# Modulation weights laid out so that each partition's share of a quarter is one contiguous row

## The reference, cut to what matters

```
def ada_params(cond_act, w, b):
    mod = cond_act @ w + b
    return jnp.split(mod, 3, axis=-1)

act_lat = jax.nn.silu(c)          # [1, 1024]
act_ctx = jax.nn.silu(c_ctx)      # [1024]
for i in range(DEPTH):            # 2 layers; w_ada[i] is [1024, 3072]
    sh_l, sc_l, gt_l = ada_params(act_lat, w_ada[i], b_ada[i])
    u_lat = rms_norm(h_lat, norm_g[i]) * (1.0 + sc_l[:, None, :]) + sh_l[:, None, :]
    sh_c, sc_c, gt_c = ada_params(act_ctx, w_ada[i], b_ada[i])
    ...
```

## Time and profile before

| | |
|---|---|
| median of 3 runs | 1286.72 us (1286.43 to 1286.76) |
| profiled execution, its own time | 1288.5 us |
| its span | 1286.7 us, 17486 instructions |
| PE busy | 1272.4 us (99%) |
| DVE / ACT / POOL busy | 64% / 51% / 35% |
| DMA | 135.44 MB in 181402 packets, mean 105 GB/s |
| in the first 40 us | 13.45 MB in 7944 packets, mean 336 GB/s |
| granted TensorE clock | 1.00 in every stretch of 40 us and of 2 us looked at |

### The profile page before, as it was taken

How to read it: one execution, slowest core, us unless ns; L and a number is a source line. 1 busy time by engine, 2 the same in 40 slices (tenths; PEclk the granted TensorE clock), 3 DMA queues, 4 the chain that set the end, 5 groups by cost and what they waited for, 6 DMA issues and landing times.

```text
span 1286.7 us, 17486 instructions
## 1 busy us (share of the span) xinstructions
PE 1272.4 (99%) x6553; PEld 1065.8 (83%) x6553; DVE 822.9 (64%) x1216; ACT 655.6 (51%) x1074; POOL 447.7 (35%) x212
## 2 busy tenths in 40 slices
PE   8999999999999999999999999999999999999998
PEld 4688888889988888888789889888888888888886
DVE  1796788764945447789658436406448668667686
ACT  4543777844523354766655534633355534545341
POOL 0234011137432394522244233344563322333310
PEclk9999999999999999999999999999999999999999
DMA  9972001066332153321223333233354243332301
GB/s 347 306 256 74 11 23 33 18 235 196 98 99 65 34 164 99 98 54 62 65 73 93 82 82 83 67 97 98 98 158 154 85 128 99 105 109 82 115 1 66
DMA packets 181402, 135.44 MB, mean 105 GB/s; under 512 B 10155, under 2 KB 154652, under 8 KB 181325
## 3 DMA queue, kind: packets, MB, share of 16 engines
q1 hardware_dynamic: 181122, 134.34, 34.5%
q10 hardware_dynamic: 202, 0.06, 0.0%
HBM read 129.66 MB, written 4.72 MB: 104 GB/s over the span
## 4 chain that ended last, share of the span: by engine, by line
PE 84%; DVE 6%; ACT 4%; DMA 3%; issue 2%; POOL 1%; SPq 0%; DVEq 0%; ACTq 0%; POOLq 0%
PE psum L2373 26%; PE psum L2375 25%; PE psum L2374 25%; PE psum L2587 2%; DMA ada_w<-in_w_ada 1%; DMA w_raw<-in_fno_w_in 1%; PE psum L2431 1%; PE psum L2575 1%; PE psum L2576 1%; DVE out_rows L2306 1%; POOL w_lo L784 1%; ACT w_hi L903 1%; DVE m_probs L2029 0%; DVE m_turned_lo L2034 0%; PE psum L2524 0%
## 5 line engine op out<-in xcount | busy, mean ns | idle before, releaser
L784 POOL TENSOR_TENSOR w_lo<-w_raw,w_hi 128x1024 fp32r<-128x1024 f32 x148 | 382.3, 2590 | 644.8 <-ACT w_hi L903 609.6
L2373 PE MATMUL psum<-u_hi,w_hi 128*128 128x512 f32 (+1 forms) x704 | 265.2, 377 | 0.5 <-DVE u_lo L1835 0.2
L2375 PE MATMUL psum<-u_hi,w_lo 128*128 128x512 f32 (+1 forms) x704 | 260.8, 371 | 0.0
L2374 PE MATMUL psum<-u_lo,w_hi 128*128 128x512 f32 (+1 forms) x704 | 260.8, 370 | 0.0
L903 ACT ACTIVATE w_hi<-w_raw 128x1024 fp32r<-128x1024 f32 x148 | 155.0, 1054 | 72.2 <-PE psum L2375 27.9
L2373 PE MATMUL psum<-y_hi,w_hi 128*128 128x512 f32 x416 | 162.2, 390 | 0.0
L2374 PE MATMUL psum<-y_lo,w_hi 128*128 128x512 f32 x416 | 161.9, 389 | 0.0
L2375 PE MATMUL psum<-y_hi,w_lo 128*128 128x512 f32 x416 | 161.9, 389 | 0.0
L2375 PEld LDWEIGHTS psum<-u_hi,w_lo 128*128 128x128 f32 x704 | 132.6, 188 | 23.2
L2373 PEld LDWEIGHTS psum<-u_hi,w_hi 128*128 128x128 f32 x704 | 132.8, 189 | 23.0 <-POOL w_lo L784 1.1
L2374 PEld LDWEIGHTS psum<-u_lo,w_hi 128*128 128x128 f32 x704 | 132.8, 189 | 21.0 <-issue 0.2
(11 more groups left out here) (511 smaller groups left out, 2597.2 us busy)
## 6 DMA issues: line engine op xcount, KB each, us to landing
w_raw<-in_w_in SPq DMA_DIRECT2D x52, 512.0 KB, 3.8
w_raw<-in_w_up SPq DMA_DIRECT2D x32, 512.0 KB, 4.1
down_set<-in_w_down SPq DMA_DIRECT2D x32, 512.0 KB, 4.8
ada_back<-in_w_ada SPq DMA_DIRECT2D x7, 2048.0 KB, 11.5
w_raw<-in_fno_w_in SPq DMA_DIRECT2D x16, 512.0 KB, 3.9
ada_w<-in_w_ada SPq DMA_DIRECT2D x3, 2048.0 KB, 15.7
w_raw<-in_mla_w_in SPq DMA_DIRECT2D x11, 512.0 KB, 5.2
w_raw<-in_mla_w_out SPq DMA_DIRECT2D x8, 512.0 KB, 3.8
```

The source lines that it names most:

```text
L784: pool.tensor_tensor(WL[:, j, :], RAW[:, j % 2, :], f(WH[:, j, :]), ALU.subtract).then_inc(lo_done, 1)
L2373: pe.matmul(out, ah, bh, start=first, stop=False, skip_group_check=more)
L2374: pe.matmul(out, ah, bl, start=False, stop=False, skip_group_check=more)
L2375: return pe.matmul(out, al, bh, start=False, stop=last, skip_group_check=more)
```

## The change

The host hands `w_ada` over in another order, so that in DRAM a quarter is 128 rows of 16 KB, one after the other, and each row is what one partition holds. `ada_weights(q)` then needs no strides. What is loaded where, in which order, by which engine, and all computation, stay as they are. Each half of quarter 0 takes 8 KB of each of the 128 rows.

```
         def _(sp):
             def ada_weights(q):
 
-                return d["w_ada"][q // 6, :, (q % 6) * T:(q % 6 + 1) * T].rearrange("(k p) n -> p k n", p=P)
+                return d["w_ada"][q // 6, q % 6]
 
@@ kernel()
         if name in vec_of:
             key = vec_of[name]
             a = a.reshape(-1, MD if key in ("q_norm", "k_norm") else P)
+        elif name == "w_ada":
+            a = _np.ascontiguousarray(a.reshape(2, KC, P, 6, T).transpose(0, 3, 2, 1, 4))
         elif a.ndim == 3 and a.shape[0] == 1:
             a = a[0]
```

## The result

| kernel | median, us | lowest to highest | runs |
|---|---|---|---|
| before, same chip | 1286.96 | 1286.43 to 1289.33 | 9 |
| after | 1289.92 | 1289.18 to 1291.61 | 9 |

The ratio is 1.0024, interval 1.0015 to 1.0032. The forecast was 1285.2 with a range of 1283.9 to 1287.2, and a chance of 0.05 on slower by over 0.2%. Of the runs of before that stand beside e1 to e4, two (1811.86 and 1975.2 us, at mean clocks of 0.65 and 0.60) are left out of the ratios. The profiled execution of after took 1289.79 us with a span of 1288.0; that of before took 1288.5 with 1286.7.

A forecast was written before the change was run, and what follows sets the result against it. PE was taken as the bound, busy 1272.4 us of a span of 1286.7, so only its transfer waits could be won. The terms -1.1 - 0.4 = -1.5 us took 1286.7 to 1285.2, range 1283.9 to 1287.2.

The forecast's parts named there:

- Flow: Quarter transfers: longer rows flow at 415 to 420 GB/s instead of 386, winning 0.38 us on quarter 0, 0.44 on each other.
- At 22.25: Start of `ada(2)`, line 2431: quarter 2 lands 0.8 to 1.7 us earlier; PE can use at most 1.48; taken as -1.1.
- Issue: SyncE's issues: fewer pieces free it, and `vec_rows` may come earlier at line 2418; taken as 0, bounds 0 and -0.6.
- The vectors wait behind long packets: Rival, beside quarter 0: nine q10 packets each wait for a long packet, at most 1.9 us; time 1286.8; chance 0.10.
- Late quarters: Around the second norm: tiles behind quarters 10 and 11 come 0.44 us earlier or more; taken as -0.4, bounds 0 and 0.5.

The follow-up runs named there:

- e1: Kernel after, but quarter 0 handed over in 2 KB pieces as before, the other eleven quarters long: 1286.40 us, ratio 0.9996 to before.
- e4: Kernel after, but quarter 0 in 4 KB rows, the other quarters in 16 KB rows: 1286.96 us, ratio 0.9999 to before.
- e8: Kernel before, with 16 KB rows for quarters 8 to 11 alone, head as before: 1287.70 us, ratio 1.0003 to before.
- e5: Kernel before once more, no edit, for a second profile: 1286.45 us, ratio 0.9996 to the other runs of before.
- e7: Kernel before (2 KB pieces for every quarter), with the thirteen vectors packed into one transfer: 1286.96 us, ratio 1.0001 to before.
- e3: Kernel after, with eight more warm-up products of constants ahead of the wait for the vectors: 1288.62 us, ratio 1.0013 to before.
- e2: Kernel before, with only quarter 0 in 8 KB rows, all other quarters in 2 KB pieces: 1290.80 us, ratio 1.0025 to before.
- e9: Kernel after, with quarter 0 in 16 KB rows too, loaded in two halves of 64 partitions each: 1298.23 us, ratio 1.0081 to before.
- e6: Kernel after, with the thirteen vectors packed into one array and loaded by one transfer: 1285.87 us, ratio 0.9989 to before.

## Why the prediction was wrong

*Flow: right.* 8 KB packets were put at 316 or 304 ns and took 315; 415 to 420 GB/s were put and 414 to 418 flowed; the issues of lines 591 to 596 came down to 0.36 to 0.61 us as foretold (SyncE is held at line 601 instead, 19.94 us for two weight tiles from 6.47 on). The Trainium skill ("DMA: Bandwidth & Descriptors", Specifications) names 512 bytes as enough for line rate; 386 GB/s with 2 KB rows and 418 with longer ones say that 8% were left.

*At 22.25: failed.* The -1.1 rested on the 1.48 us at line 2431 of the earlier trace rows. The landing moved even further than put in this pair of traces, 2.4 us, but PE came later than the weights. And the wait itself was a trait of one execution, in which quarter 2 landed at 22.2: with the same head e8 starts `ada(2)` at 20.92 without a wait, e5 has none either, and e7, which gets to `ada(2)` earlier, waits 0.39. The profiled execution's own time was 1.8 us above the median, which the prediction wrote down and then only subtracted. That was the sign: a gain of 1.1 us was being read out of an execution that was itself 1.8 too long.

*Issue, "Taken as 0, bounds 0 and -0.6": failed, and decisively.* It looked at line 2418 from one side only. The other side stood among the rivals, *The vectors wait behind long packets*, with nine packets at 0.22 = 1.9 us; measured were steps of 0.32 us in place of 0.09, nine of them from 9.6 us on, and 1.9 to 2.1 us at line 2418 in after (1.4 in e3, 2.6 in e2, against e5). So the rival had mechanism and place right and the size of the vectors' delay too, with some luck in the number of turns, and a chance of 0.10 was too little for it. What spoke against it, that fewer pieces would let the nine go first, had no row behind it. q10 shows the opposite: 7 and 2 packets were left from 9 to 10 and from 10 to 12, and in after, in the same stretches and from 12 to 13, it is 8, 7 and 2:

```profile
q10 hardware_dynamic: 8, 0.00, 0.9%
...
q10 hardware_dynamic: 7, 0.00, 0.3%
```

The rule cited there (the Trainium skill, "DMA: Bandwidth & Descriptors", Queues, rings and completion order: an engine takes the next queue after a whole packet) agrees with these runs where a packet is one contiguous row: the steps in the table under e9 are one row long, from 2 KB to 16 KB. It says nothing of the number of turns, and that varied.

*The clock: not in the sum at all; failed.* The rival priced its late `ada(0)` at 7.03 us. But PE stands idle for 2.65 us there, and `ada(0)` took 8.48; e3 gives 1.3 us for the clock by the whole time. With it the rival would have come to 1286.8 + 1.45 = 1288.25, beyond the range; the 1.48 us of wait at line 2431, which it let absorb most of the delay, and that e5 and e8 don't have, is nearly the rest of the way to 1289.92.

*Late quarters: likely right in sign, mis-sized.* -0.4 with a bound of 0.5, measured -0.9 between the two traces; over all traces the two lengths of row overlap (see e8). The transfers sped up as in after's chain, where the 10.72 us at 298.35 have no successor and one of 3.91 at 314.32 is the longest; but PE's listed waits were no bound for it, and the 0.3 at line 2667 stayed. From the last product of line 2587 to the end of line 2667 (268.3 to 322.1 in before, 270.5 to 323.4 in after) the same 356 products take 53.80 us and 52.90, so all of the 0.9 is in this stretch. Idle time is only 0.67 - 0.41 = 0.26 of it; the other 0.64 is in time that the profile counts as busy (53.13 against 52.49). PE's weight loads of line 2373 waited 0.4 us for `u_lo` and 0.3 for `w_lo` in before and for neither in after: waits that the list of PE itself shows only in part, 0.2.

*The sum by the runs.* `ada(2)` at 24.45 in after and at 20.92 in an undisturbed head of before (e8): +3.5. Less 0.9, if the late stretch gives that: +2.6, against +2.96 between the medians. By parts: 1.9 for the vectors' turns (13.02 against 11.13 in e8), 1.45 and 0.2 for the clock in `ada(0)` and in the twelve transposes (1.67 against 1.48).

## What to carry to other kernels

Before rows of a transfer are made longer, list what other queues have in flight beside it and what waits for that: each small packet that is left waits for one long packet at each turn, here six to eleven times 0.23 us more than before, and the larger rate pays back 8% of the transfer. Pack the small ones into one transfer first; in e6 the long rows then harmed nothing. A wait of the size of the hoped-for gain, read from one profiled execution that lies above the median, is to be seen in a second one before a sum rests on it, and a new idle stretch of PE is to be charged with the clock behind it.

## What was not expected of the hardware

Beside long packets on one queue, small packets of another moved at one per long packet, 0.32 us apart with 8 KB rows and 1.29 with the slow 16 KB ones of e9. A transfer to 64 partitions ran at 188 GB/s in e9 where one to 128 partitions ran at 418. The clock's fall is not the same from run to run of one kernel: in e5 PE was idle 1.21 us before 9.45 and 0.61 before 11.15 and the clock fell, in e8 1.11 and 0.88 and it did not; in after, with 2.65 us idle in its trace, the mean clock was under 1.00 in all nine runs. And PE's list of waits is not a ceiling for what a stretch can give: 0.5 us listed, 0.9 less between the two traces, with 0.7 of waits in the list of its weight loads.
